# The last pair of four 256-column projections written to two PSUM banks, its first tile evicted and squared apart

## The reference, cut to what matters

```python
y = jnp.concatenate([y_conv, y_ret], axis=-1) @ w_out[i]      # phase "out"
x = x + rmsnorm(y, mix_post_norm[i])                          # norm "post1"
f = (silu(h @ w_ffn_gate[i]) * (h @ w_ffn_up[i])) @ w_ffn_down[i]   # phase "dn"
x = x + rmsnorm(f, ffn_post_norm[i])                          # norm "fpost1"
h = h + g_m * y            # y: last product with wo, phase "wo1"; then rmsnorm(h): norm "f1"
h = h + g_f * swiglu(...)  # last product with w_down, phase "dn1"; then rmsnorm(h): norm "final"
```

## Time and profile before

| what | value |
|---|---|
| median of 3 runs | 1465.03 us (1462.82 to 1466.31) |
| the profiled execution's own time | 1463.84 us |
| its span, first to last instruction | 1462.0 us |
| TensorE busy | 1412.3 us (97% of the span) |
| GpSimd busy | 852.5 us (58%) |
| VectorE busy | 703.5 us (48%) |
| ScalarE busy | 608.7 us (42%) |
| mean granted TensorE clock | 0.982 |

### The profile page before, as it was taken

How to read it: one execution, slowest core, us unless ns; L and a number is a source line. 1 busy time by engine, 2 the same in 40 slices (tenths; PEclk the granted TensorE clock), 3 DMA queues, 4 the chain that set the end, 5 groups by cost and what they waited for, 6 DMA issues and landing times.

```text
span 1462.0 us, 25926 instructions
## 1 busy us (share of the span) xinstructions
PE 1412.3 (97%) x9210; PEld 1262.0 (86%) x9210; DVE 703.5 (48%) x1313; ACT 608.7 (42%) x972; POOL 852.5 (58%) x426
## 2 busy tenths in 40 slices
PE   8998999999899999799999999999999999999998
PEld 7998999999787888587888888888888788999997
DVE  5884555556724645735655655344324383311111
ACT  6346554454533444534322323222332265454452
POOL 4784688888546665341543533544374452688895
PEclk8999999999999999999999999999999999999999
DMA  7643477786321222021565565635293101455563
GB/s 291 230 151 99 172 277 278 268 297 225 123 86 58 87 73 87 15 96 52 202 213 185 184 215 175 217 132 178 69 256 116 44 10 63 133 183 186 175 213 101
DMA packets 83195, 227.27 MB, mean 155 GB/s; under 512 B 23872, under 2 KB 29248, under 8 KB 82880
## 3 DMA queue, kind: packets, MB, share of 16 engines
q1 hardware_dynamic: 82688, 224.91, 45.8%
q10 hardware_dynamic: 448, 1.57, 0.5%
HBM read 222.26 MB, written 1.05 MB: 153 GB/s over the span
## 4 chain that ended last, share of the span: by engine, by line
issue 38%; POOL 30%; PE 27%; DVE 1%; ACT 1%; POOLq 1%; SPq 0%; DMA 0%; DVEq 0%; ACTq 0%
POOL wl L526 26%; PE ps L1025 6%; PE ps L1027 6%; PE ps L1026 6%; PE ps L1088 1%; PE ps L1089 1%; PE ps L1090 1%; PE ps L1362 1%; PE ps L1288 1%; POOL xl L560 1%; PE ps L1112 1%; PE ps L1309 1%; PE ps L1376 1%; PE ps L1098 1%; PE ps L1354 1%
## 5 line engine op out<-in xcount | busy, mean ns | idle before, releaser
L526 POOL TENSOR_TENSOR wl<-raw,wh 128x1024 fp32r<-128x1024 f32 x310 | 742.5, 2416 | 542.4 <-ACT wh L627 542.3
L1025 PE MATMUL ps<-xh,wh 128*128 128x256 f32 (+1 forms) x1728 | 563.2, 326 | 15.5 <-POOL wl L526 8.1
L1026 PE MATMUL ps<-xl,wh 128*128 128x256 f32 (+1 forms) x1728 | 556.5, 322 | 0.0
L1027 PE MATMUL ps<-xh,wl 128*128 128x256 f32 (+1 forms) x1728 | 556.3, 322 | 0.0
L627 ACT ACTIVATE wh<-raw 128x1024 fp32r<-128x1024 f32 x310 | 318.6, 1053 | 283.7 <-PE ps L1027 182.3
L1025 PEld LDWEIGHTS ps<-xh,wh 128*128 128x128 f32 x1728 | 331.8, 192 | 50.3 <-POOL wl L526 11.3
L1027 PEld LDWEIGHTS ps<-xh,wl 128*128 128x128 f32 x1728 | 331.7, 192 | 23.8
L1026 PEld LDWEIGHTS ps<-xl,wh 128*128 128x128 f32 x1728 | 332.0, 192 | 22.5
L1025 PE MATMUL ps<-fh,wh 128*128 128x256 f32 (+1 forms) x528 | 168.9, 320 | 1.7 <-POOL wl L526 1.7
L1027 PE MATMUL ps<-fh,wl 128*128 128x256 f32 (+1 forms) x528 | 168.7, 320 | 0.0
L1026 PE MATMUL ps<-fl,wh 128*128 128x256 f32 (+1 forms) x528 | 168.7, 320 | 0.0
(11 more groups left out here) (222 smaller groups left out, 1650.4 us busy)
## 6 DMA issues: line engine op xcount, KB each, us to landing
raw<-wall SPq DMA_DIRECT2D x310, 512.0 KB, 3.7
ada_late<-wada SPq DMA_DIRECT2D x56, 512.0 KB, 3.4
ada<-wada SPq DMA_DIRECT2D x40, 512.0 KB, 3.4
bias<-rpb SPq DMA_DIRECT2D x16, 256.0 KB, 6.8
h<-xin SPq DMA_DIRECT2D x2, 1024.0 KB, 7.2
sww<-qk SPq DMA_DIRECT2D x32, 64.0 KB, 2.0
csb<-cond SPq DMA_DIRECT2D x1, 1024.0 KB, 8.0
sw<-u ACTq DMA_DIRECT2D x2, 512.0 KB, 6.7
```

The costliest lines, as they stand in the source:

```text
L526: nc.gpsimd.tensor_tensor(wl[:, slot, :, :], raw[:, slot, :, :], wh[:, slot, :, :].bitcast(F32), ALU.subtract).then_inc(lo_ready, 1)
L1025: nc.tensor.matmul(o, wa, xa, start=start, stop=False, skip_group_check=True)
L1026: nc.tensor.matmul(o, wa, xb, start=False, stop=False, skip_group_check=True)
L1027: return nc.tensor.matmul(o, wb, xa, start=False, stop=stop, skip_group_check=True)
```

## The change: the last pair in two banks

In the four phases named in `APART` the last pair goes to two banks: its first tile to bank 1, its second to bank 0, each in columns 0 to 255. Before the first product of the second tile TensorE waits until pair 2 has left bank 0. When the last product of the first tile is done TensorE raises `half_done`; ScalarE and VectorE then take the first tile and, when the pair is done, the second. The order of the products is the same. The four phases have their last iteration written out behind the loop, and the fillers of their norms write bank 4 up to the transposes; the counts of fillers are unchanged.

```diff
+APART = ("out", "dn", "wo1", "dn1")
+        def apart_bank(o):
+            return ps[:, 1 - o, 0:SEQ]
     square_pair:
+                if src is None and p == 3:
+                    for o in range(2):
+                        if o == 0:
+                            act.wait_ge(S("half_done"), 1 + APART.index(ph.name))
+                        else:
+                            pair_done(act, ph, 0, p)
+                        nc.scalar.activation(new[:, o, :], apart_bank(o), ACT.Square)\
+                            .then_inc(S("sq_new"), 1)
+                    return
-                elif n == NT and p == 3:
+                elif p == 3 and name != "ple1":
                     for o in range(2):
                         if o == 0:
-                            act.wait_ge(S("tile_ready"), 1 + (name == "m1"))
+                            act.wait_ge(S("tile_ready"), 1 + ("f0", "m1", "f1", "final").index(name))
     features:
+                apart = n == SEQ and ph.name in APART
+                        last = apart and (i, pair) == (1, 1)
+                                    if last and o == 1 and k == 0:
+                                        pe.wait_ge(bank_free, ph.pair0 + 5)
-                                    mm = three(tile_bank(pair, o, n, wide), ...
+                                    mm = three(apart_bank(o) if last else tile_bank(pair, o, n, wide), ...
+                                if last and o == 0 and k == ktiles - 1:
+                                    mm.then_inc(S("half_done"), 1)
-                run(pe, ph, body, ph.iters - 1 if within else 0)
+                run(pe, ph, body, ph.iters - 1 if within or apart else 0)
     norm_sum:
-                    keep_busy(waiting[0], 0)
+                    spare_bank = 4 if SUMMED[name] in APART and n == SEQ else 0
+                    keep_busy(waiting[0], spare_bank)
-                    keep_busy(waiting[1], 1 if name == "fpre1" else 0)
+                    keep_busy(waiting[1], spare_bank if name in SUMMED else 1 if name == "fpre1" else 0)
     take_summed:
+                    if p == 3:
+                        for o in range(2):
+                            dve.wait_ge(S("sq_new"), 8 * list(SUMMED).index(norm) + 2 * p + o + 1)
+                            ins = V.tensor_scalar(dst[:, 2 * p + o, 0:SEQ], apart_bank(o), 1.0, None, ALU.mult)
+                        ins.then_inc(bank_free, 1)
+                        break
     take_gated:
-                    pair_done(dve, ph, 0, p)
+                    halves = n == SEQ and p == 3
                     for o in range(2):
+                        if halves and o == 0:
+                            dve.wait_ge(S("half_done"), 1 + APART.index(ph.name))
+                        elif halves or o == 0:
+                            pair_done(dve, ph, 0, p)
...
+                            bank = apart_bank(o) if halves else tile_bank(p % 2, o, n)
-                        if n == NT and p == 3 and o == 0:
+                        if p == 3 and o == 0:
                             ins.then_inc(S("tile_ready"), 1)
```

More of the change, by code:

```diff
@@ L1048, in body @@
                                         pe.wait_ge(S(sem), n0 + each * (k + 1))
-                                    mm = three(tile_bank(pair, o, n, wide), wh[:, slot, kk, c], wl[:, slot, kk, c],
-                                               a[:, k, 0:n], b[:, k, 0:n], k == 0 and (n == NT or wide or o == 0), k == ktiles - 1)
+                                    if last and o == 1 and k == 0:
+                                        pe.wait_ge(bank_free, ph.pair0 + 5)
+                                    mm = three(apart_bank(o) if last else tile_bank(pair, o, n, wide),
+                                               wh[:, slot, kk, c], wl[:, slot, kk, c], a[:, k, 0:n], b[:, k, 0:n],
+                                               k == 0 and (n == NT or wide or last or o == 0), k == ktiles - 1)
+                                if last and o == 0 and k == ktiles - 1:
+                                    mm.then_inc(S("half_done"), 1)
                             mm.then_inc(units_done, 1)
-                run(pe, ph, body, ph.iters - 1 if within else 0)
+                run(pe, ph, body, ph.iters - 1 if within or apart else 0)
             def tokens(ph, tiles):
@@ L1642, in take_gated @@
                             row = section(l, 2 + 3 * w) + k
-                            ins = V.scalar_tensor_tensor(h[:, k, t], tile_bank(p % 2, o, n)[:, t], mod[:, l, row, c:c + 1],
+                            bank = apart_bank(o) if halves else tile_bank(p % 2, o, n)
+                            ins = V.scalar_tensor_tensor(h[:, k, t], bank[:, t], mod[:, l, row, c:c + 1],
                                                          h[:, k, t], ALU.mult, ALU.add)
-                        if n == NT and p == 3 and o == 0:
+                        if p == 3 and o == 0:
                             ins.then_inc(S("tile_ready"), 1)
```

## The result

The changed kernel takes 1467.01 us in the median of 14 runs (1464.26 to 1469.62), the kernel before 1464.21 us in 14 runs (1462.06 to 1467.63). The ratio is 1.0017, 95% interval 1.0009 to 1.0025: 2.5 us slower, within 1.3 to 3.7 us; the two medians lie 2.8 us apart. The forecast was +2.0 us and 1467.0 us. The profiled execution took 1467.07 us, span 1465.3 us.

The account below looks back on a forecast made before the run. TensorE, busy 97% of the span, was taken as the bound, so a pause in a last pair costs its full length; 1.31 + 1.89 - 0.59 - 0.59 = +2.02 us on 1465.03 gave 1467.0 us, range 1463.8 to 1470.0.

Parts of the forecast that it names:

- the four places: "out" and "dn" were to lose 1.31 and 1.89 us, "f1" and "final" to gain 0.59 us each.
- the sum of the places: Whole kernel: 1.31 + 1.89 - 0.59 - 0.59 = +2.02 us, added to 1465.03 us.
- Not measurably: Whole kernel: a little slower, but within 0.2% (2.9 us), about what a measurement can't tell from none; chance 0.66.
- The new wait in "out" and "dn": Before the last pair's thirteenth product TensorE waits for pair 2 to leave bank 0; costs 1.31 and 1.89 us.
- the stall with the transfer in time: In "dn", if the weight copy ahead of the square need not wait 0.32 us for its transfer: 1.57 us.
- No wait in "wo1" and "dn1": Last pairs: bank 0 is free 0.25 and 0.22 us before the thirteenth product; cost 0, at worst 0.10 us each.
- Nothing gained in "post1" and "fpost1": Behind the last product the 8 fillers end last and their number is unchanged; gain 0.
- 0.59 us in "f1" and in "final": Behind the last product only the second tile is left to square; 2.85 us fall to 2.26 in each.
- The loops: "out", "dn" and "dn1" lose a jump by the written-out iteration; nothing gained or lost.
- Rival A: Pause in "dn" or "out" halves the granted clock, 1.5 us per stretch; 1468.5 to 1470.0 us; chance 0.15.
- The same price from a shift of the later work against the clock's changes: Later work: 1.5 us, with either sign, as part of the clock rival; chance 0.15 for that rival.
- Rivals B and C: B: bank wait met in time or won back, 1463.9 us, chance 0.09; C: tail gain absent, 1468.4 us, chance 0.10.

Follow-up runs that it names:

- e9: The changed kernel once more, unedited, timed beside the kernel before: 1467.29 us, ratio 1.0008 (0.9996 to 1.0021).
- e8: The changed kernel with 9 filler products ahead of the wait for pair 2 in "out" and "dn": 1467.5 us, ratio 1.0009 to the kernel before.
- e2: The kernel before with the change in "out" and "dn" only: 1469.03 us, ratio 1.0027 (1.0014 to 1.0039).
- e6: The changed kernel, bank wait kept, with fewer fillers (none in "post1" and "fpost1", 4 in "f1" and "final"): 1463.04 us, ratio 0.9986 to the kernel before.
- e4: The changed kernel with the second tile of "out" and "dn" in unheld bank 4, without the wait: 1462.27 us, ratio 0.9986 to the kernel before.
- e5: e4 with fewer fillers (none in "post1" and "fpost1", 4 in "f1" and "final"): 1461.83 us, ratio 0.998 to the kernel before.
- e7: The kernel before, without split, with fewer fillers (none in "post1" and "fpost1", 4 in "f1" and "final"): 1464.94 us, ratio 1.0005.
- e1: The kernel before with the change in "wo1" and "dn1" only: 1461.9 us, ratio 0.9987 (0.9977 to 0.9996).
- e3: The kernel before with only the last iteration of "out", "dn" and "dn1" written out behind the loop: 1463.93 us, ratio 0.9993 (0.9981 to 1.0005).

## Why the prediction was right

The sign, the four places and the releasers came as forecast. That the median of 1467.01 us meets the forecast 1467.0 us to the digit is luck: the sum was added to a median of three runs, 1465.03 us, that lies 0.8 us above the later one of fourteen, and the sum of the places was +1.60 us in place of +2.02. "Not measurably" was too careful: fourteen runs of each give an interval that excludes 1.

**The new wait in "out" and "dn"**: right in place, releaser and size in "out" (1.32 for 1.31 us). In "dn" 1.44 us for 1.89. The mis-sized part is how late the copy ahead of the square starts: in the trace of before 0.83 us after the last pair's first product (340.03 - 339.20), in the changed kernel 0.37 us after it (340.55 - 340.18). The forecast put the stall with the transfer in time at 1.57 us, still above what came, because it took off only the copy's own wait of 0.32 us. ScalarE's copy before that one had waited for its transfer too, started at 338.64 and ended inside the pair; in the changed kernel it started at 339.01 and ended before the pair began. The thirteenth product of "dn" was late by 1.34 us in the changed kernel, 1.22 in e9, 1.24 in e8, 1.54 in e2 and 1.74 in e6, against the forecast 1.79: the term was read from one execution in which transfers were late, and stands at the top of what came. e4 shows the cause by taking the wait away.

**No wait in "wo1" and "dn1"**: right. Both last pairs keep 5.76 and 15.67 us. VectorE left bank 0 at 1253.15 and 1440.73 us, 0.29 and 0.28 us ahead of the thirteenth product.

**Nothing gained in "post1" and "fpost1"**: right, 2.05 for 2.04 us, with the reason given there, fillers that end last; e5 and e7 show that reason.

**0.59 us in "f1" and in "final"**: right, 0.58 each; the rows of e1 show it alone.

**The loops**: nothing was forecast, and e3 finds no difference it can resolve. The stall behind a taken branch that the Trainium skill describes ("Runtime: NRT & Kernel Launch", Instruction fetch mechanics) shows as a gap in no row here; the rule is for a target outside the fetched window, and no run shows whether these loops' targets were.

**Rival A, the clock**: not needed for the loss, but not the outsider that I made of it, and not ruled out as a part. The granted clock stays 1.00 in all four last pairs. The argument that the wait of 2.60 us in "out" was followed by full pace was weak: it was one execution. In e4, at the same wait in the same place, the clock did fall. TensorE at that wait and, from 2.0 us behind it, a stretch in e4, then the same stretch of the kernel before, whose clock is 1.00 from 104 to 150 us:

```profile
128.96 0.36 PE L1042 MATMUL ps<-xh,wh 128*128 128x256 f32 x1 [2.69 <-POOL wl L534]
131.00:134.20 3.20, 3.20 (x18) 3.20 (x18) 0.72 (x2) 0.80 (x1) 3.20 (x3) 0.57 0.62 236
```

```profile
131.00:134.20 3.20, 3.20 (x29) 3.20 (x28) 1.65 (x4) 1.19 (x3) 3.20 (x2) 1.00 0.52 164
```

18 products in place of 29 in the same 3.2 us. "The same price from a shift of the later work against the clock's changes" is what the profiled execution shows in "pg", 1.34 us. It is one of the pieces by which the span is 3.3 us longer where the four places give 1.60; the others have both signs. The ratio over all runs, +1.3 to +3.7 us, holds the 1.60 us as well as the forecast 2.02 us, so how much of the median is the clock's is open.

**Rivals B and C**: the wait was not met in time and not won back (e2 lost all of it), and the tail gain came in full.

## What to carry to other kernels

Before a tile is moved to a bank that another tile has just left, compare two moments in the trace: when its first product would start, and when the old tenant's last reader ends. Here the bank came free 1.2 to 1.7 us too late where a square stands ahead of the eviction, and 0.3 us in time where it does not; a bank without a tenant removed the cost. Look at more than one execution where that moment hangs on a transfer. And before the work behind the last product is made shorter, look at what ends last there: where it is a fixed number of filler instructions, the gain only comes when their number goes down with it. Take them out only where nothing else leaves the engine waiting in their place: without the split the waits came back and, in the execution profiled, the clock fell behind two of the norms.

## What the runs showed of the hardware that I had not expected

A fall of the granted clock costs or not by what comes next. The same phase took 37.94 us with its slow stretch ahead of a wait of TensorE and 39.28 us with it behind. Two executions of the changed kernel itself show the free case. In the second (e9) the clock was 0.50 from 123 to 126 us, in the first it was 1.00 there, and yet the next weight unit released TensorE at the same time. Only the wait ahead of it is shorter:

```profile
130.41 0.36 PE L1039 MATMUL ps<-xh,wh 128*128 128x256 f32 x1 [2.69 <-POOL wl L531]
130.44 0.35 PE L1039 MATMUL ps<-xh,wh 128*128 128x256 f32 x1 [1.22 <-POOL wl L531]
```

Two profiled executions can so differ by more than a microsecond in a stage that no edit touched, and one place (the wait of 2.6 us in "out") is followed by full clock in one kernel's execution and by half clock in another's.
